# Two causal convolution layers on one core: where the low parts of the weights are made, and which engine takes which taps

## The reference

```python
def conformer_conv_mixer(h, w_in, conv_w, conv_b, ln_g, ln_b, w_out):
    proj = h @ w_in                              # 1024 -> 3 * 2048
    val, glu_gate, z = jnp.split(proj, 3, axis=-1)
    u = val * jax.nn.sigmoid(glu_gate)
    u = causal_depthwise_conv(u, conv_w) + conv_b    # 31 taps
    u = jax.nn.silu(layer_norm(u, ln_g, ln_b))
    return (u * jax.nn.silu(z)) @ w_out
```

## Time and profile before

| what | value |
| --- | --- |
| median of 3 runs (lowest, highest) | 2704.99 us (2704.19, 2705.07) |
| the profiled execution | 2705.57 us, span 2703.8 us |
| busy, share of the span | TensorE 96%, VectorE 58%, ScalarE 41%, GpSimd 56% |
| chain that ended last, by engine | TensorE 76%, VectorE 17%, ScalarE 3% |
| mean granted TensorE clock | 0.982 |
| transfers | 236.63 MB, 88 GB/s |

### The profile page before, as it was taken

One profiled execution on the slowest core, in us unless ns is written; L12 is line 12 of the kernel. 1 busy time (PEld: TensorE's weight loads), 2 busy tenths in 40 slices (PEclk: granted clock), 3 DMA queues, 4 the chain that ended last, 5 costly groups with the idle time before them and its releaser, 6 DMA issues.

```text
span 2703.8 us, 31508 instructions
## 1 busy us (share of the span) xinstructions
PE 2600.4 (96%) x12172; PEld 2094.8 (77%) x12172; DVE 1574.6 (58%) x2509; ACT 1113.0 (41%) x1787; POOL 1526.5 (56%) x846
## 2 busy tenths in 40 slices
PE   8999899999999999999999999989999999999998
PEld 7777677877777777888888777768877778788887
DVE  4999975135856833444450799988488764432202
ACT  3454544335554633222232455544335554332322
POOL 3798856444444355544455489766634537544652
PEclk9999999999999999999999999989999999999999
DMA  4232223543344323333333222212421233232231
GB/s 120 78 85 75 91 70 81 103 94 65 77 78 66 79 67 90 95 104 98 94 94 106 67 78 78 78 63 98 128 95 63 88 104 121 79 109 94 94 105 51
DMA packets 267541, 236.63 MB, mean 88 GB/s; under 512 B 16181, under 2 KB 240655, under 8 KB 267392
## 3 DMA queue, kind: packets, MB, share of 16 engines
q1 hardware_dynamic: 264240, 223.94, 30.0%
q0 software_dynamic: 3152, 10.68, 1.3%
HBM read 228.75 MB, written 5.84 MB: 87 GB/s over the span
## 4 chain that ended last, share of the span: by engine, by line
PE 76%; DVE 17%; ACT 3%; issue 2%; POOL 2%; DMA 0%; DVEq 0%; POOLq 0%; ACTq 0%
PE ps L64 73%; DVE ps L81 8%; DVE AR L81 4%; PE ps L67 2%; DVE AR L73 2%; DVE HL L81 1%; ACT L70 1%; POOL AR L73 1%; ACT AR L70 1%; POOL WL L73 1%; ACT HT L70 1%; DVE X L73 1%; DVE ST L97 0%; DMA AR<-in_x 0%; DVE AR L77 0%
## 5 line engine op out<-in xcount | busy, mean ns | idle before, releaser
L73 POOL TENSOR_TENSOR WL<-WR,WH 128x1024 fp32r<-128x1024 f32 (+1 forms) x405 | 1007.8, 2510 | 856.9 <-ACT WH L70 856.9
L64 PE MATMUL ps<-HH,WH 128*128 128x512 f32 x3080 | 1230.7, 400 | 24.4 <-POOL WL L73 15.1
L64 PE MATMUL ps<-HL,WH 128*128 128x512 f32 x3080 | 1205.6, 391 | 0.0
L64 PE MATMUL ps<-HH,WL 128*128 128x512 f32 x3080 | 1205.5, 391 | 0.0
L64 PEld LDWEIGHTS ps<-HH,WH 128*128 128x128 f32 x3080 | 582.5, 189 | 168.6 <-issue 35.4
L64 PEld LDWEIGHTS ps<-HL,WH 128*128 128x128 f32 x3080 | 583.0, 189 | 123.0 <-issue 6.7
L64 PEld LDWEIGHTS ps<-HH,WL 128*128 128x128 f32 x3080 | 582.1, 189 | 124.0
L70 ACT ACTIVATE WH<-WR 128x1024 fp32r<-128x1024 f32 (+1 forms) x405 | 403.9, 1046 | 465.8 <-PE ps L64 454.6
L81 DVE SCALAR_TENSOR_TENSOR ps<-AR,CW,ps 128x512 f32<-128x512 f32 x732 | 505.2, 755 | 10.4 <-ACT ps L70 3.0
L70 ACT ACTIVATE AR<-ps 128x512 f32<-128x512 f32 (+3 forms) x265 | 132.6, 524 | 413.9 <-PE ps L64 314.4
L73 DVE TENSOR_TENSOR AR<-AR 128x512 f32<-128x512 f32 (+1 forms) x161 | 226.6, 1436 | 38.7 <-ACT AR L70 37.1
(11 more groups left out here) (167 smaller groups left out, 2012.8 us busy)
## 6 DMA issues: line engine op xcount, KB each, us to landing
WR<-in_a_w_in SPq DMA_DIRECT2D x64, 512.0 KB, 5.1
WR<-in_c_w_in SPq DMA_DIRECT2D x64, 512.0 KB, 5.3
WR<-in_a_w_in SPq DMA_DIRECT2D x16, 1024.0 KB, 5.3
WR<-in_a_w_out SPq DMA_DIRECT2D x16, 1024.0 KB, 4.8
WR<-in_b_w_in SPq DMA_DIRECT2D x16, 1024.0 KB, 8.4
WR<-in_b_w_in SPq DMA_DIRECT2D x32, 512.0 KB, 13.4
WR<-in_w_mlp_in SPq DMA_DIRECT2D x16, 1024.0 KB, 5.4
WR<-in_w_mlp_out SPq DMA_DIRECT2D x16, 1024.0 KB, 4.9
```

The lines of the kernel that those rows point to most:

```text
L64: return Op(None if self.e is None else self.e.matmul(o, l, r, start=first, stop=last, skip_group_check=True))
L73: return Op(None if self.e is None else self.e.tensor_tensor(o, a, b, op))
```

## The change

- A chunk of gate and value columns now has the gate's first, and its two halves lie one behind the other in `WR`, `WH` and `WL` (1024 columns each) where they were interleaved; z chunks come in two transfers. TensorE takes half 0 for the gate.
- `summed` names 38 halves a layer: both halves of the fifteen gate/value chunks behind the first, and half 0 of the eight z chunks. For these ScalarE also writes the negated rounded weights into `WL`, and GpSimd issues a transfer from `WR` to `WL` that adds (`accum_op`). A reader of the low part waits for that transfer's semaphore (`wait_low`). The other halves are subtracted on GpSimd as before.
- `gemm_low_last`: 16 matmuls with the high part, then the wait, then the 8 with the low part. It takes the place of `gemm` for all gate and value products but slot 0's and for z 0 to 14.
- ScalarE splits half 1 of the next chunk at the slot's start and half 0 of the one behind it after the sigmoid. From slot 2 on it does starts, evacuations, chain starts and half of the slot's products ahead of the sigmoid and the other half behind it. GpSimd's order follows.
- `POOL_TAPS` has channels 2, 4, 7 and 10 fully and 18 taps of channel 12. By the plan VectorE has 333 taps a layer (366 before), GpSimd 138 adds (104). The plan has 15 taps, later 7, and 7 or 8 adds, later 3, in a slot.
- z 13 is made in slot 31, ahead of the last transposes.

```diff
+
+    def dma_add(self, o, i):
+        return Op(None if self.e is None else self.e.dma_start(o, i, accum_op=ALU.add))
...
         def layer_a_chunks(j):
             FIRST_A[j] = len(specs)
             for i in range(KE):
-                cols(a_w_in[j], (i * P, P), (E + i * P, P), used=(a_val, j, i))
+                first_free[len(specs)] = (a_gate, j, i)
+                cols(a_w_in[j], (E + i * P, P), (i * P, P), used=(a_val, j, i))
             for i in range(KE // 2):
-                cols(a_w_in[j], (2 * E + 256 * i, 256), used=(a_z, j, 2 * i + 1))
+                first_free[len(specs)] = (a_z, j, 2 * i)
+                cols(a_w_in[j], (2 * E + 256 * i, P), (2 * E + 256 * i + P, P), used=(a_z, j, 2 * i + 1))
...
+        def two_runs(i):
+
+            return specs[i][0] == "in" and [n for _, n in specs[i][2]] == [P, P]
+
...
+            if two_runs(i):
+                return [t[:, n * 1024:(n + 1) * 1024].rearrange("p (k c) -> p k c", k=8) for n in range(2)]
...
+
+        w_sum = [[sig(f"w_sum{i}{n}") for n in range(2)] for i in range(2)]
+
+        def summed(i, n):
+
+            return any(f < i < f + KE + (KE // 2 if n == 0 else 0) for f in FIRST_A)
+
+        def wait_low(eng, i, n):
+            if summed(i, n):
+                eng.wait_ge(w_sum[i % 2][n], i)
+            else:
+                eng.wait_ge(w_lo, i, n)
...
             if before:
-                sp.wait_ge(w_lo, before[-1], len(halves(WR, before[-1])) - 1)
+                for n in range(len(halves(WR, before[-1]))):
+                    wait_low(sp, before[-1], n)
...
-        def split_hi(act, i):
+        def split_hi(act, i, which=(0, 1)):
+
             if i < len(specs):
                 for n, (r, h) in enumerate(zip(halves(WR, i), halves(WH, i))):
+                    if n not in which:
+                        continue
                     act.wait_ge(w_landed[i % 2], i, -1)
                     if i >= 2:
-                        act.wait_ge(*specs[i - 2][3])
+                        act.wait_ge(*(first_free[i - 2] if n == 0 and i in first_free and i - 2 in first_free else specs[i - 2][3]))
                     act.act(h, r, ACT.Copy).then_inc(w_hi, i, n)
-
-        def split_lo(pool, i):
+                    if summed(i, n):
+                        act.act(halves(WL, i)[n], r, ACT.Copy, scale=-1.0).then_inc(w_hi, i, n, "low")
+
+        def split_lo(pool, i, which=(0, 1)):
             if i < len(specs):
                 for n, (r, h, l) in enumerate(zip(halves(WR, i), halves(WH, i), halves(WL, i))):
-                    pool.wait_ge(w_hi, i, n)
-                    pool.tt(l, r, h, ALU.subtract).then_inc(w_lo, i, n)
+                    if n not in which:
+                        continue
+                    if summed(i, n):
+                        pool.wait_ge(w_hi, i, n, "low")
+                        pool.dma_add(l.rearrange("p k c -> p (k c)"), r.rearrange("p k c -> p (k c)")).then_inc(w_sum[i % 2][n], i, by=16)
+                    else:
+                        pool.wait_ge(w_hi, i, n)
+                        pool.tt(l, r, h, ALU.subtract).then_inc(w_lo, i, n)
...
+        def gemm_low_last(pe, i, half, o, gen):
+
+            wh, wl = halves(WH, i)[half], halves(WL, i)[half]
+            pe.wait_ge(w_hi, i, half)
+            for k in range(8):
+                wait_h(pe, gen, k)
+                pe.mm(o, wh[:, k, :], hs(HH, k), k == 0, False)
+                pe.mm(o, wh[:, k, :], hs(HL, k), False, False)
+            wait_low(pe, i, half)
+            for k in range(8):
+                op = pe.mm(o, wl[:, k, :], hs(HH, k), False, k == 7)
+            return op
...
-        POOL_TAPS = {2: PAD, 4: PAD, 9: PAD, 10: 14}
+        POOL_TAPS = {2: PAD, 4: PAD, 7: PAD, 10: PAD, 12: 18}
...
-                room = PAD * KE if rest else 15 + (slot >= 3) if slot < KE else 8
+                room = PAD * KE if rest else (15) if slot < KE else (7)
...
-                room = PAD * KE if rest else 5 + slot % 2 if slot < KE else 2 + slot % 2
+                room = PAD * KE if rest else (7 + slot % 2) if slot < KE else (3)
...
+            o = banks[(2 + n) % 3][:, :]
+            if n == KE - 1:
+                gemm(pe, FIRST_A[j] + KE + n // 2, 1, o, 3 * j, (a_z, j, "last")).then_inc(a_z, j, n)
+            else:
+                gemm_low_last(pe, FIRST_A[j] + KE + n // 2, n % 2, o, 3 * j).then_inc(a_z, j, n)
...
-                    gemm(pe, c0 + slot, 1, banks[2 * slot % 3][:, :], gen).then_inc(a_gate, j, slot)
+                    product = gemm_low_last if slot else gemm
+                    product(pe, c0 + slot, 0, banks[2 * slot % 3][:, :], gen).then_inc(a_gate, j, slot)
                     if slot:
                         pe.wait_ge(a_sig, j, slot - 1)
-                    gemm(pe, c0 + slot, 0, banks[(2 * slot + 1) % 3][:, :], gen).then_inc(a_val, j, slot)
+                    product(pe, c0 + slot, 1, banks[(2 * slot + 1) % 3][:, :], gen).then_inc(a_val, j, slot)
                 elif slot < 2 * KE - Z_LATE:
                     z_tensor(pe, j, slot - KE)
+                elif slot == 2 * KE - 1:
+                    z_tensor(pe, j, KE - 3)
...
             for i in LATE_TURN:
                 turn_u(pe, j, i)
-            z_tensor(pe, j, KE - 3)
...
-        def conv_scalar(act, j, at):
-            if at["start"]:
-                products_scalar(act, j, at)
+        def conv_scalar(act, j, at, some):
+            starts_scalar(act, j, at)
             for i in at["evac"]:
                 evacuate_scalar(act, j, i)
...
-            if not at["start"]:
-                products_scalar(act, j, at)
-
-        def products_scalar(act, j, at):
+            products_scalar(act, j, some)
+
+        def starts_scalar(act, j, at):
...
             for slot in range(2 * KE + 1):
+                n = PLAN[slot]["add"]
                 if slot < KE:
-                    split_hi(act, c0 + slot + 1)
+                    split_hi(act, c0 + slot + 1, (0, 1) if slot == 0 else (1,))
+                    if slot >= 2:
+                        conv_scalar(act, j, PLAN[slot], n[:len(n) // 2])
                     act.wait_ge(a_gate, j, slot)
                     if slot >= 2:
                         act.wait_ge(a_u, j, slot - 2)
                     act.act(SIG[slot % 2], banks[2 * slot % 3][:, :], ACT.Sigmoid).then_inc(a_sig, j, slot)
+                    split_hi(act, c0 + slot + 2, (0,))
+                    if slot < 2:
+                        conv_scalar(act, j, PLAN[slot], [])
+                    products_scalar(act, j, n[len(n) // 2:])
                 elif slot < 2 * KE - Z_LATE:
+                    m = (slot - KE) // 2
                     if slot % 2 == 0:
-                        split_hi(act, c0 + KE + (slot - KE) // 2 + 1)
+                        split_hi(act, c0 + KE + m + 1, (1,))
+                    elif m + 2 < KE // 2:
+                        split_hi(act, c0 + KE + m + 2, (0,))
                     silu_z(slot - KE)
-                conv_scalar(act, j, PLAN[slot])
+                    conv_scalar(act, j, PLAN[slot], n)
+                else:
+                    conv_scalar(act, j, PLAN[slot], n)
...
             for slot in range(2 * KE + 1):
+                n = PLAN[slot]["add"]
                 if slot < KE:
-                    split_lo(pool, c0 + slot + 1)
-                elif slot < 2 * KE - 2 and slot % 2 == 0:
-                    split_lo(pool, c0 + KE + (slot - KE) // 2 + 1)
-                conv_gpsimd(pool, j, PLAN[slot])
+                    split_lo(pool, c0 + slot + 1, (0, 1) if slot == 0 else (1,))
+                    conv_gpsimd(pool, j, n[:len(n) // 2])
+                    split_lo(pool, c0 + slot + 2, (0,))
+                    conv_gpsimd(pool, j, n[len(n) // 2:])
+                else:
+                    m = (slot - KE) // 2
+                    if slot < 2 * KE - Z_LATE and slot % 2 == 0:
+                        split_lo(pool, c0 + KE + m + 1, (1,))
+                    elif slot < 2 * KE - Z_LATE and m + 2 < KE // 2:
+                        split_lo(pool, c0 + KE + m + 2, (0,))
+                    conv_gpsimd(pool, j, n)
```

More of the change, by code:

```diff
@@ L206, in build_program @@
         specs = []
+        first_free = {}
         def cols(w, *runs, used):
@@ L323, in load_chunk @@
                 for n, (c0, width) in enumerate(runs):
-                    sp.dma(dst[:, :, o:o + width], src[:, :, c0:c0 + width]).then_inc(
+                    to = halves(WR, i)[n] if two_runs(i) else dst[:, :, o:o + width]
+                    sp.dma(to, src[:, :, c0:c0 + width]).then_inc(
                         w_landed[i % 2], i, n - len(runs), by=16)
@@ L352, in wait_h @@
             pe.wait_ge(hl_p if gen in (0, 3) and k % 2 else hl_v, gen, k)
+        def gemm_low_last(pe, i, half, o, gen):
[9 more added lines that the diff above has]
+            return op
         def gemm(pe, i, half, o, gen, last=None):
-            pe.wait_ge(w_lo, i, half)
+            wait_low(pe, i, half)
```

(17 more changed lines are left out.)

## The result

The changed kernel takes 2718.36 us (median of 4 runs, 2716.69 to 2719.83) against 2704.59 before (4 runs, 2703.59 to 2705.07): a ratio of 1.0051, 95% interval 1.0034 to 1.0069. It is slower by 13.8 us where 23 us less were forecast.

A forecast was written before the change was run, and what follows sets the result against it. TensorE was taken to pace slots 6 to 15, VectorE's taps to set the layer's end. The last reading at 330 instead of 341.6 gave 2 x 11.7 = 23.4 us off 2705.57: 2682, range 2655 to 2722.

The forecast's parts named there:

- Slot 5's taps end at 129.3 and slot 6 repeats the pattern, sigmoid until 133: TensorE, ready at 128.6, loses 4.4: ScalarE's order, slot 6: the late sigmoid delays TensorE 4.4 us at slot 7's value product; gate 8 ends at 145.7.
- Slots 9 to 15: TensorE behind ScalarE's sigmoids: slot 9 costs 1.5 us more, slots 11 and 13 nothing; gate 15 ends at 235.7.
- rival (3): Sigmoid behind the evacuation stalls every slot that has one, some 3 us each, 9 to 12 a layer: 2700 to 2710; chance 0.14.
- 22 to 26 us less: VectorE: 333 taps instead of 366 shorten its work by this much a layer; 11.7 us of it come through.
- z 13: Moved from behind the last turn to slot 31 on TensorE: between 1.5 us less and 2 more, booked 0.
- The layer's end: TensorE, not VectorE, comes last: z 12 at 322.7, z 13 at 328.1, last reading at 330 instead of 341.6.
- ScalarE fits: ScalarE's second passes (40 us a layer) and 35 more products (22) leave a slot 10.1 us of work in some 12.3.
- Rival (1): GpSimd's issues of accumulating transfers are dear, deciding from 1.7 us each; 2749 at 2.42 us an issue; chance 0.12.
- 309: When GpSimd's work ends in the layer, at 0.58 us an issue; under TensorE's 329, so booked 0.
- Landing: Time for an accumulating transfer to land: 5 us, ends 4.8 and 10; a sum may take 10; booked 0.
- rival (2): Sums land late: from 10 us raw buffers turn slower than slots; at 15 us a landing, 2767; chance 0.08.
- Rival (4): ScalarE is never late: gate 15 ends some 13 us earlier than forecast, VectorE's gain comes through whole, 2655; chance 0.13.

The follow-up runs named there:

- e10: The changed kernel, sigmoid still behind the evacuation, but in slots 0 to 15 VectorE reads a turn's statistics ahead of its gate multiply: 2705.28 us (1.0004).
- e2: The changed kernel with z 13 put back behind the last transpose: 2714.95 us (1.0040 to before).
- e6: The kernel before with only z 13 moved forward to slot 31, ahead of the last transposes: 2710.9 us (1.0026).
- e9: The changed kernel with ScalarE's and GpSimd's order of before; sums, moved taps and early z 13 stay: 2691.86 us (0.9955 to before).
- e9z: The changed kernel with ScalarE's and GpSimd's order of before and z 13 behind the last transpose; sums and moved taps stay: 2691.26 us (0.9953).
- e1: The changed kernel with the sigmoid, and also the split of half 0 two chunks ahead, put in front of all convolution work on ScalarE: 2725.9 us (1.0081).
- e5b: The changed kernel with ScalarE's and GpSimd's order of before, z 13 behind, all low parts subtracted on GpSimd, 33 taps moved: 2731.40 us (1.0101).
- e4b: The changed kernel with ScalarE's and GpSimd's order of before, z 13 behind and the taps of before (366), sums kept: 2702.46 us (0.9993).
- e8: The changed kernel with only the sigmoid of slots 2 to 15 moved ahead of starts, evacuations, chain starts and first products: 2696.08 us (0.9973).

## Why the prediction was wrong

**The step that failed** is ScalarE's, "Slot 5's taps end at 129.3 and slot 6 repeats the pattern, sigmoid until 133: TensorE, ready at 128.6, loses 4.4". The sigmoid came at 131.82 to 132.4, as said. But TensorE didn't get to the value product of slot 7: it stood from 124.3 in front of the turn of slot 7, 9.7 us, because VectorE reads the turn before only behind its gate multiply. The wait for the sigmoid was followed to the gate multiply and the value product, not to what VectorE has queued **behind** the multiply, though the earlier trace rows had just these turns as TensorE's largest wait. With the stretch 130 to 140 granted 0.60 of 2.4 GHz, part of it at 1.2, gate 8 ended 8.9 us late. e10, which cuts this one link, gives 13.1 us back. That 2718.36 lies inside 2655 to 2722 is luck: the upper end stood for dear issues and late landings, and neither came.

**Slots 9 to 15** were right on TensorE: gate 8 to gate 15 was forecast at 90.0 us and took 88.2 (154.6 to 242.8), and TensorE waits 1 us between 140 and 250; the 1.5 us of slot 9 didn't come. "Slots 11 and 13 nothing" holds for TensorE, not for VectorE: in slots 9 and 13 it loses 1.2 and 3.0 us more in front of the multiply. So rival (3), whose time of 2700 to 2710 was nearest, had the right place, the sigmoid behind the evacuation, but not the right way: no stall in every such slot, one long one and VectorE's losses.

**VectorE.** "22 to 26 us less" is all but right: the taps are busy 231.0 us, 252.6 before. The forecast had VectorE's taps end at 320; they end at 335.6, since 21 us of new waits took the place of the work. The forecast counted three losses, 10.5 us, which measured 10.2; slots 9 and 13 and 7.0 us of waits for turns were not in it.

**z 13** at 0 was mis-sized: e2 and e6 show 3.4 and 7.1 us. It was priced at the work that it had beside it, not at what it stands in front of; in the order of before with the new taps it is indeed worth 0.6, within the spread.

**The layer's end** was forecast at 330 and came at 347.1: 8.9 us late at gate 8, less 1.8 gained up to gate 15, is 7.1; 3.3 more up to z 12 (333.1 for 322.7); and 6.7 behind it, as the turns had to wait for VectorE's reading at 335.6, with z 13, 6.3 us, between that and the last two. The 3.3 could have been seen in the earlier trace rows: from the end of gate 15 to that of z 12 the kernel before took 91.3 us and the changed one 90.3, but the sum has 87.0 for it. A wait for ScalarE at the start of chain 15, 1.9 us (1.3 before), has no term there; the rest is open.

**ScalarE fits** in its slots: shown, as in e9 it waits for no load and TensorE waits for it 1.9 us.

**GpSimd.** The issue was taken at 0.58. GpSimd's rows of the changed kernel:

```profile
90.46 0.87 POOL L115 DMA_DIRECT2D WL<-WR  x1
91.06 2.98 POOL L73 TENSOR_TENSOR AR<-AR,SQ 128x512 f32<-128x512 f32 x2
```

The next instruction starts 0.60 us behind the issue, though its record lasts 0.87. The Trainium skill (DMA: Bandwidth & Descriptors, section Latency and other measured facts) has about 1 us to the first byte of such a transfer for the core's work; of that, GpSimd's program sees 0.60 here. Rival (1), from 1.7 us on, is out. But "309" for GpSimd's end was far off: 341.3 in the changed kernel, 331.2 in e9z. It was worked out as if GpSimd never waited from 131 on; it waits 31.3 us for ScalarE, nearly all of it for products, behind 120 us, 23.0 in e9z, and 309 + 23 is 332. The margin under TensorE was not there: in e9z TensorE's turn waits 4.5 us for this add, some 9 in both layers where 23.4 were forecast as won. No run takes that wait away alone.

**Landing** was booked at 5 us: 5.1 median, 4.4 to 9.9. TensorE waits for no summed part in the changed kernel, 3.1 us in e9z: rival (2) is out. Mis-sized was the reload, 4.8 for what is 8.1 to 10.7 in e1; the changed kernel has room for it (ScalarE waits 9.6 us for loads), e1 had not.

**Rival (4)**, ScalarE never late, is e9: its premise nearly holds (TensorE waits 1.9 us for ScalarE) and its 2655 does not: gate 15 ends at 230.3, 5 us and not 13 earlier than forecast, and the taps end at 324.2, but the last reading at 335.6, so that VectorE's gain doesn't come through whole even there. Of the tests named ahead, "333 taps", "landing under 10", no wait for a low part and the three waits of VectorE came true, and "issues of 0.5 to 1.2 us" by the 0.60 us from an issue to the next start, though their records last up to 1.8; "the last reading ending near 330" did not (347.1), nor z 12's silu near 323 (333.2), and "TensorE waiting for ScalarE's sigmoid in slots 5 and 7" did in slot 5 alone.

## What to carry to other kernels

When an instruction is made later on one engine, follow it through each engine's program order: what stands behind the first instruction that waits for it, and who waits for that; here a statistics reading behind a multiply cost more than the multiply's own reader did. Work that is freed on one engine pays only if the engine that sets the end gets it in the same change, and an order that lets a plain, often-awaited result wait behind a bulky one can eat more than both. An end time of a helping engine must be summed with its waits, not from its durations alone.

## What the runs showed of the hardware

An accumulating transfer of 512 KB from SBUF to SBUF with 128 rows lands in 5.1 us, as fast as a plain load of that size from HBM in the same kernel (5.2), though an addition takes two inputs. The Trainium skill (DMA: Bandwidth & Descriptors, section Anatomy of one DMA) fits transfers issued from GpSimd with 2 us and the bytes at 436 KB a us, which makes an estimate of 3.2 us; the measured 5.1 holds here.

The profile by windows of the changed kernel, the busiest stretch of slots:

```profile
120.00:250.00 130.00, 119.26 (x499) 92.50 (x498) 111.63 (x183) 95.82 (x146) 112.52 (x96) 0.96 0.71 163
```

The DMA engines' share is 0.71, 0.27 in e5b without the sums, and yet the median of plain loads of 512 KB went from 4.8 to 5.2 us only. The slowest tell more, in the part with the convolution: 6.3 us before and 6.2 in e5b, both without sums, but 9.4 to 10.8 in the changed kernel, e1, e4b, e8, e9 and e9z. GpSimd's adds start 1.25 us apart where they follow one another, as before, though their records are longer (1.56 us in the mean, 1.29 before).
